# State tiles of a state-space mixer in pairs, the rotation table finished earlier, and modulation pieces in other buffers

## The chip, the cores and the metric

One core of a Trainium2 chip runs the whole program. The metric is the device time of one execution in microseconds, the median over several runs. The profile is of one execution; times in it count from the first instruction of the span.

## The reference

Two blocks run one after the other on `x` (256 tokens by 1024 features, float32). Each has two layers, and each layer a mixer and a feed-forward part, both modulated by six vectors `mod = silu(c) @ mod_w + mod_b`. The change touches the first layer of the first block alone:

```
mod = silu(c) @ mod_w[0] + mod_b[0]            # sh1, sc1, g1, sh2, sc2, g2
h = modulate(rms_norm(x, g), sh1, sc1)
proj = h @ ab_w_in                             # u (512), q, k, v (512 each)
# state-space mixer on u: 32 groups of 16 features, 64 complex states each
bu = einsum(u, b_bar)                          # per state, complex
x_t = a * x_{t-1} + bu_t                       # complex a, over 256 tokens
y = Re(einsum(x, c)) + d * u
y = gelu(y);  y_ssm = y * sigmoid(y @ glu_w + glu_b)
# attention on q, k, v: 8 heads of 64, causal, with a bias table
y = concat(y_ssm, y_att) @ ab_w_out
x = x + g1 * y
```

Everything is computed in float32. Large products are made from a rounded upper part and a rest of each operand (`w_hi`, `w_lo`, `h_hi`, `h_lo`), three matmuls for each product; `ab_in` alone is done with plain float32 matmuls.

## The kernel before

All weights come as a stream of chunks of 128 by 2048 through three `raw` buffers, filled by DMAs that SyncE issues. ScalarE makes `w_hi` (function `hi`, L746) and VectorE `w_lo` (`lo`, L1368) of each chunk, TensorE multiplies. The first eight chunks (`ab_in`) are used straight from `raw`. Chunk 8 is glu, chunks 9 to 12 are ab_out, and then the feed-forward part follows. Each engine's order is written out by hand; semaphores tie them.

**State tiles.** The 2048 complex states lie in 16 tiles of 128 (`j` = 0 to 15). The recurrence with a complex factor is done as a real scan in a frame that turns: `turns_[:, j]` is the table of cosines and sines (`e_re`, `e_im`) of 256 steps for the tile. It is built by doubling: 64 steps for all tiles at the start, then for each tile 64 to 128 (`BASE`) and 128 to 256 (`2 * BASE`), each time two ScalarE copies (`twist`, L884 and L885) and one VectorE instruction (`double`, L1625). For a tile TensorE makes the input (`bu`, L2318, with 32 rows of contraction: row group `j % 4`) into bank `j % 2`; VectorE turns it (`ssm_tile`, L1656 to L1660), scans (L1662) and turns back (L1671, L1673) into `by_cos[j % 2]` and `by_sin[j % 2]`; TensorE takes it through C (`y_of`, L2335, 32 output rows: column group `j % 4`) and adds up in `Y_BANK`, with a skip product (L2329) at every fourth tile. A plain float32 matmul shows as two records. Tiles 0 to 7 have four terms in `y_of`. From tile 8 on GpSimd makes the `by_sin` product (L728) and VectorE combines the parts (`turned_back`, L1682 and L1683), so that two terms remain.

**Order.** In the loop over the 8 chunks of ab_in, TensorE does chunk `c`, `bu(c + 1)` and `y_of(c - 2)`; ScalarE copies chunk `c` out of its bank (L921), converts chunk `c + 3` where that is 8 or more, and twists; VectorE does the conversion's rest, a double, `ssm_tile(c)` and another double. In the loop over 8 heads TensorE does `bu(9 + h)`, `y_of(7 + h)`, the turn of the previous head's probabilities (L2136), the modulation pieces of this head (L2213), the previous head's output (L2397) and the next head's scores (L2377); VectorE does `ssm_tile(8 + h)` with doubles, the reciprocal of the previous head (L1702), this head's bias and maximum (L1693, L1696) and `turned_back`; ScalarE twists, scales the previous head's probabilities (L933), takes the exponential (L961) and copies (L939, L944). Behind the last head ScalarE copies the last part of y (`y_out`, L906), does gelu (L973) and the upper part for the glu product (L976), and TensorE opens the glu banks (L2304).

**Modulation pieces.** `mod` of this layer is 48 pieces of 128 by 1024 (`pm_piece`, L2213), four column groups of 32 at once. Pieces 0 to 15 run before ab_in. Pieces 16 to 47 are loaded into the halves of the three `raw` buffers (6 slots, `pm_late`) after ab_out 0 and 1 have been converted, and used in heads 1 to 7, five for each head (`late_pieces`). Then SyncE goes on with chunk 11.

Of the kernel before, what the change touches and what calls it, by code (L numbers as in the profile page):

```python
# [18 lines left out]
F32 = mybir.dt.float32  # L19
# [53 lines left out]
PM_SLOTS, PM_LATE = 8, 6  # L73
# [184 lines left out]
def build(nc, A, out):  # L258
    with ExitStack() as ctx:
# [12 lines left out]
        w_hi = [sb(f"w_hi{i}", [P, CHUNK], F32R) for i in range(SLOTS)]  # L272
        w_lo = [sb(f"w_lo{i}", [P, CHUNK], F32R) for i in range(SLOTS)]
        x = sb("x", [P, 2, D])
        h_hi, h_lo = sb("h_hi", [P, DT, T], F32R), sb("h_lo", [P, DT, T], F32R)
# [53 lines left out]
        by_cos, by_sin = ([at(PREP + 3072 + 1024 * k + 512 * i, 2, T) for i in range(2)] for k in range(2))  # L329
# [6 lines left out]
        pm_late = [raw[i // 2][:, i % 2 * PM_COLS:(i % 2 + 1) * PM_COLS] for i in range(PM_LATE)]  # L336
# [130 lines left out]
        for m in range(PM_PIECES):  # L467
            k = m % PM_SLOTS if m < PM_FIRST else (m - PM_FIRST) % PM_LATE
# [22 lines left out]
        Y_BANK = (2, 6, 2, 5)  # L491
        DOUBLED = [(j, BASE) for j in range(4)] + [(j, 2 * BASE) for j in range(2)]
        for _c in range(8):
            DOUBLED += [(_c + 4, BASE), (_c + 2, 2 * BASE)]
        for _h in range(6):
            DOUBLED += [(_h + 12, BASE)] * (_h < 4) + [(_h + 10, 2 * BASE)]
# [74 lines left out]
        def _(sp):  # L571
# [48 lines left out]
            def load_pm(m):  # L620
# [3 lines left out]
                n = PM_LATE if first else PM_SLOTS  # L624
                if m >= first + n:
                    sp.wait_ge(sem("pm_used"), m - n + 1)
# [17 lines left out]
            load_plain("ab_in", 2, 6)  # L644
# [6 lines left out]
            sp.wait_ge(hi_done, Q["ab_out"] + 2 - PLAIN)  # L651
            sp.wait_ge(lo_done, Q["ab_out"] + 2 - PLAIN)
            for h in range(1, HEADS):
                for m in late_pieces(h):
                    load_pm(m)
                if h <= 4:
                    load_bias(h + 3)
            sp.wait_ge(sem("pm_used"), PM_PIECES)
# [65 lines left out]
        def _(pool):  # L724
            for j in range(8, ST):
                pool.wait_ge(sem("scan_done"), j - 7)
                pool.wait_ge(*((sem("state_ready"), j - 1) if j >= 10 else (sem("ssm_y_done"), j - 1)))
# [2107 lines left out]
```

## Time and profile before

| | us |
|---|---|
| device time, median of 3 runs | 1533.94 (1531.2 to 1534.71) |
| the profiled execution's time | 1535.15 |
| its span, first to last instruction | 1533.3 |
| TensorE matmuls busy | 1441.6 (94% of the span) |
| VectorE busy | 1089.6 (71%) |
| ScalarE busy | 773.2 (50%) |
| GpSimd busy | 19.6 (1%) |

A busy time is the time in which an engine had an instruction in work; matmuls are pipelined, and their records overlap. A record of the timeline has a start, a length, the engine, the line and the tiles; in brackets stands the idle time of the engine before it and who ended it. The granted clock (PEclk) is TensorE's clock as a share of 2.4 GHz; its low level is 0.5.

### The profile page before, as it was taken

How to read it: one execution, taken by the hardware profiler on the slowest of the kernel's cores; microseconds unless marked ns; L12 is line 12 of the kernel's file. 1: busy time of each engine (PE TensorE's matmuls, PEld its weight loads, DVE VectorE, ACT ScalarE, POOL GpSimd, SP SyncE). 2: the span in 40 equal slices, each digit the busy share in tenths (PEclk: the TensorE clock that was granted, in tenths of full speed). 3: DMA queues.
4: the chain of work that ended last, by engine and by line, in shares of the span. 5: the costliest groups of instructions: out<-in, count | busy, mean ns of one | idle time of the engine just before them, and what ended most of it. 6: DMA issues, size and time to landing. Idle time of an engine off the chain costs nothing.

```text
span 1533.3 us, 24753 instructions
## 1 busy us (share of the span) xinstructions
PE 1441.6 (94%) x9349; PEld 1196.7 (78%) x9363; DVE 1089.6 (71%) x1664; ACT 773.2 (50%) x1142; POOL 19.6 (1%) x14
## 2 busy tenths in 40 slices
PE   6996789999999999999999889999999999999998
PEld 3772458899976668999979755799997877799997
DVE  6657746988894465998985467586667859676666
ACT  4123355545554265555555667565446542455554
POOL 0001100000000000000001000000000000000000
PEclk9996899999999999999999999999999999999999
DMA  9434644888869774898833400355555434345551
GB/s 367 143 108 165 227 183 175 344 326 307 318 245 358 304 290 190 344 370 313 344 147 114 144 6 19 135 192 171 199 178 180 178 110 137 110 165 191 179 198 61
DMA packets 58059, 315.63 MB, mean 206 GB/s; under 512 B 7011, under 2 KB 8524, under 8 KB 33856
## 3 DMA queue, kind: packets, MB, share of 16 engines
q1 hardware_dynamic: 54114, 304.35, 53.7%
q10 hardware_dynamic: 3870, 10.25, 2.2%
q8 instruction: 51, 0.84, 0.2%
q14 instruction: 24, 0.20, 0.0%
HBM read 311.85 MB, written 1.15 MB: 204 GB/s over the span
## 4 chain that ended last, share of the span: by engine, by line
PE 76%; DVE 9%; ACT 5%; issue 5%; DMA 4%; SPq 0%; ACTq 0%; DVEq 0%; POOL 0%
PE bank L2263 60%; PE bank L2356 3%; PE bank L2536 2%; PE bank L2136 2%; ACT w_hi L746 1%; DMA raw<-in_stream 1%; PE bank L2213 1%; DMA arena<-in_mod_pe 1%; DVE w_lo L1368 1%; PE bank L2620 1%; PE bank L2154 1%; DMA arena<-in_mod_later 1%; DVE hf L1524 1%; ACT hf L786 1%; DVE arena L1396 1%
## 5 line engine op out<-in xcount | busy, mean ns | idle before, releaser
L1368 DVE TENSOR_TENSOR w_lo<-raw,w_hi 128x2048 fp32r<-128x2048 f32 x178 | 407.3, 2289 | 180.5 <-ACT w_hi L746 179.6
L2263 PE MATMUL bank<-h_hi,w_hi 128*128 128x256 f32 x1704 | 487.2, 286 | 2.2 <-ACT arena L1229 0.9
L2263 PE MATMUL bank<-h_lo,w_hi 128*128 128x256 f32 x1704 | 482.0, 283 | 0.0
L2263 PE MATMUL bank<-h_hi,w_lo 128*128 128x256 f32 x1704 | 482.0, 283 | 0.0
L746 ACT ACTIVATE w_hi<-raw 128x2048 fp32r<-128x2048 f32 x178 | 340.6, 1914 | 135.7 <-PE bank L2263 110.3
L2263 PEld LDWEIGHTS bank<-h_hi,w_hi 128*128 128x128 f32 x1704 | 326.8, 192 | 9.2 <-issue 4.1
L2263 PEld LDWEIGHTS bank<-h_lo,w_hi 128*128 128x128 f32 x1704 | 326.7, 192 | 2.3 <-issue 0.7
L2263 PEld LDWEIGHTS bank<-h_hi,w_lo 128*128 128x128 f32 x1704 | 326.7, 192 | 0.0
L1786 DVE SCALAR_TENSOR_TENSOR arena<-bank,par,arena 128x255 f32<-128x255 f32 (+1 forms) x264 | 109.1, 475 | 111.0 <-ACT arena L1017 79.3
L2263 PE MATMUL bank<-w_hi,a_hi 128*128 128x512 f32 x368 | 146.0, 397 | 5.0 <-DVE a_lo L1811 4.2
L2263 PE MATMUL bank<-w_hi,a_lo 128*128 128x512 f32 x368 | 144.2, 392 | 0.0
L2263 PE MATMUL bank<-w_lo,a_hi 128*128 128x512 f32 x368 | 143.9, 391 | 0.0
L1017 ACT ACTIVATE arena<-bank,par 128x256 f32<-128x256 f32 x88 | 44.8, 559 | 139.1 <-PE bank L2263 139.1
L1396 DVE SCALAR_TENSOR_TENSOR arena<-arena,silu_c 128x384 f32<-128x384 f32 (+1 forms) x192 | 104.3, 612 | 0.0
L2263 PEld LDWEIGHTS bank<-w_hi,a_hi 128*128 128x128 f32 x368 | 69.5, 189 | 22.2 <-DVE w_lo L1368 5.2
L2263 PE MATMUL bank<-w_hi,h_hi 128*128 128x512 f32 x192 | 76.9, 401 | 5.8 <-DVE hf L1524 3.0
L2263 PEld LDWEIGHTS bank<-w_lo,a_hi 128*128 128x128 f32 x368 | 69.5, 189 | 15.1
L2263 PEld LDWEIGHTS bank<-w_hi,a_lo 128*128 128x128 f32 x368 | 69.7, 189 | 12.9
L2263 PE MATMUL bank<-w_lo,h_hi 128*128 128x512 f32 x192 | 75.3, 392 | 0.0
L2263 PE MATMUL bank<-w_hi,h_lo 128*128 128x512 f32 x192 | 75.3, 392 | 0.0
L2136 PEld LDWEIGHTS bank<-ident_sb,hf 128*128 128x128 f32 x304 | 38.9, 156 | 36.6 <-ACT hf L933 15.8
L2136 PE MATMUL bank<-ident_sb,hf 128*128 128x128 f32 x304 | 47.2, 303 | 19.6 <-ACT hf L933 13.1
(328 smaller groups left out, 1752.7 us busy)
## 6 DMA issues: line engine op xcount, KB each, us to landing
raw<-in_stream SPq DMA_DIRECT2D x186, 1024.0 KB, 5.0
arena<-in_mod_stream SPq DMA_DIRECT2D x64, 768.0 KB, 8.0
arena<-in_mod_later SPq DMA_DIRECT2D x48, 512.0 KB, 7.8
raw<-in_mod_pe SPq DMA_DIRECT2D x40, 512.0 KB, 6.4
arena<-in_mod_pe SPq DMA_DIRECT2D x8, 512.0 KB, 10.0
sq<-row_store ACTq DMA_DIRECT2D x7, 512.0 KB, 3.8
sq<-in_bias SPq DMA_DIRECT2D x8, 256.0 KB, 5.8
x<-in_x_t ACTq DMA_DIRECT2D x1, 1024.0 KB, 8.8
```

The lines of the kernel that those rows point to most:

```text
L746: nc.scalar.activation(w_hi[s][:], raw[s][:], ACT.Copy).then_inc(hi_done, 1)
L786: nc.scalar.activation(hf[:, k, :], turned(n, k), ACT.Identity, **by).then_inc(sem("full_ready"), 1)
L1017: ins = nc.scalar.activation(gate_c[:, e, :], half(4, e), ACT.Identity, scale=par[:, bass.ds(wb[center] + 2 * s + e, 1)], bias=par[:, bass ...
L1368: nc.vector.tensor_tensor(w_lo[s][:], raw[s][:], w_hi[s][:].bitcast(F32), ALU.subtract).then_inc(lo_done, 1)
L1396: ins = nc.vector.scalar_tensor_tensor(parts[e], buf[:, kt % 4, :], silu_c[:, c0 + kt:c0 + kt + 1], parts[e], ALU.mult, ALU.add)
L1524: ins = nc.vector.tensor_tensor(part, acc[:], row_at(gate_rows[gate], fh), ALU.mult)
L1786: ins = nc.vector.scalar_tensor_tensor(o, src, par[:, bass.ds(w[tap] + 2 * s + e, 1)], o, ALU.mult, ALU.add)
L2136: return nc.tensor.transpose(out_, in_, ident[0:n, 0:n])
L2154: nc.tensor.matmul(bank[dst][:], zeros[:, 0:P], zeros[:], start=True, stop=True)
L2263: ins = nc.tensor.matmul(out_, l, r, start=first and n == 0, stop=last and n == 2, **kw)
L2356: ins = nc.tensor.matmul(half(4 + fill % 2, n), *sides, start=c > 0 and k == 0, stop=k == DT - 1, skip_group_check=c == 0)
L2536: ins = nc.tensor.matmul(bank[2 * part + ft][:], dft[:, part, t, ft * P:(ft + 1) * P], sources[part][:, t, 512 * s_:512 * s_ + 512], start ...
```

## The change

- Pieces 16 to 47 go into 8 slots that lie on the memory of `w_hi[0]`, `w_lo[0]`, `w_hi[1]` and `w_lo[1]`. Pieces 16 to 23 are loaded already behind chunk 2 of ab_in, and run in head 0; four follow in each of heads 1 to 6. The conversions of chunks 9 and 10 (ab_out) wait until the pieces are through: ScalarE does them ahead of head 7's probabilities, VectorE behind head 7. Chunk 8 (glu) is converted by ScalarE behind ab_in and by VectorE in head 6.
- The doublings are done in seven steps of four, all within ab_in, by `TWISTS_BEHIND` on ScalarE and `DOUBLE_AHEAD` on VectorE.
- `bu` and `y_of` become `bu_pair` and `y_pair`: two tiles with their instructions in turn, so that neighbours are in different row groups or column groups. The inputs lie in banks 0 and 1, or 3 and 7. Ten tiles are computed in ab_in, the rest in heads 0 to 5.
- GpSimd's product and `turned_back` go; each tile has both products on VectorE and four terms. `by_cos` and `by_sin` have four buffers each; two of them lie on the memory of `h_hi`.

```diff
+        with ExitStack() as early:
+            early_pieces = [early.enter_context(nc.sbuf_tensor(f"early_pieces{i}", [P, CHUNK], F32)) for i in range(4)]
+            early_states = early.enter_context(nc.sbuf_tensor("early_states", [P, DT, T], F32))
+        w_split = [sb(("w_hi", "w_lo")[i % 2] + str(i // 2), [P, CHUNK], F32R) for i in range(4)]
+        h_hi = sb("h_hi", [P, DT, T], F32R)
...
         def late_pieces(h):
-            return range(PM_FIRST + 5 * max(h - 1, 0), min(PM_FIRST + 5 * h, PM_PIECES))
+            first = PM_FIRST + (0, 8, 12, 16, 20, 24, 28, 32)[h]
+            return range(first, min(first + (4 if h else 8), PM_PIECES))
...
+        EARLY = 10
+        BU_BANKS = ((0, 1), (3, 7), (0, 1), (3, 7), (0, 1), (0, 1), (0, 1), (0, 1))
+        BU_BEFORE = (None, None, 0, 1, 2, 4, 5, 6)
+        def doublings(s):
+            return [(j, BASE) for j in range(4 + 2 * s, min(6 + 2 * s, ST))] + [(j, 2 * BASE) for j in (2 + 2 * s, 3 + 2 * s)]
+        TWISTS_BEHIND = {0: (0,), 1: (1,), 3: (2,), 4: (3, 4), 5: (5, 6)}
+        DOUBLE_AHEAD = {1: 0, 3: 1, 5: 2, 6: 3, 7: 4, 8: 5, 9: 6}
...
@@ SyncE @@
-            load_plain("ab_in", 2, 6)
+            load_plain("ab_in", 2, 3)
+            for m in late_pieces(0):
+                load_pm(m)
+            load_plain("ab_in", 3, 6)
...
-            sp.wait_ge(hi_done, Q["ab_out"] + 2 - PLAIN)
-            sp.wait_ge(lo_done, Q["ab_out"] + 2 - PLAIN)
-            for h in range(1, HEADS):
+            for h in range(HEADS - 1):
                 for m in late_pieces(h):
-                    load_pm(m)
...
+                    if m + PM_SLOTS < PM_PIECES:
+                        load_pm(m + PM_SLOTS)
-            sp.wait_ge(sem("pm_used"), PM_PIECES)
...
@@ GpSimd @@
-            for j in range(8, ST):
-                pool.wait_ge(sem("scan_done"), j - 7)
-                nc.gpsimd.tensor_tensor(by_sin[j % 2], rot_b, e_im[:, j, :].unsqueeze(1).broadcast_to([P, 2, T]), ALU.mult)\
...
@@ VectorE @@
+                if j >= 4:
+                    dve.wait_ge(sem("ssm_y_done"), j // 2 - 1)
+                nc.vector.tensor_tensor(by_cos[j % 4], rot_b, er, ALU.mult)
+                nc.vector.tensor_tensor(by_sin[j % 4], rot_b, ei, ALU.mult).then_inc(sem("state_ready"), 1)
...
+            for j in range(EARLY):
+                if j in DOUBLE_AHEAD:
+                    for jj, m in doublings(DOUBLE_AHEAD[j]):
+                        double(jj, m)
+                ssm_tile(j)
             for h in range(HEADS):
+                if h + EARLY < ST:
+                    ssm_tile(h + EARLY)
+                if h == HEADS - 2:
+                    lo_upto(Q["glu"])
                 if h:
                     recip(h - 1)
                 head(h)
+            lo_upto(Q["ab_out"] + 1)
...
@@ TensorE, chunk loop @@
+                if c in (2, 3, 5, 6, 7):
+                    y_pair((2, 3, 5, 6, 7).index(c))
+                if c == 2:
+                    pe.wait_ge(bank_free, FILL["ab_in"] + 2)
+                if c in (2, 3, 4, 6):
+                    bu_pair(2 + (2, 3, 4, 6).index(c))
...
@@ TensorE, head loop @@
+                if h in (1, 3):
+                    bu_pair(6 + h // 2)
                 if h + 1 < HEADS:
                     scores(h + 1)
+                if h in (1, 3, 5):
+                    y_pair(5 + h // 2)
```

## Rows read from the trace of the kernel before

**Rows 1.** Windows: busy us (instructions) of each engine, POOL, granted clock, DMA share, GB/s.
```profile
0.00:38.00 38.00, 24.48 (x170) 11.53 (x172) 26.39 (x113) 15.72 (x40) 0.21 (x4) 1.00 0.94 366
34.00:115.00 81.00, 78.95 (x348) 59.43 (x348) 48.80 (x85) 18.92 (x48) 0.00 (x0) 1.00 0.40 142
115.00:130.00 15.00, 7.33 (x20) 3.12 (x20) 11.62 (x19) 4.70 (x11) 0.52 (x1) 0.66 0.48 180
130.00:144.00 14.00, 9.13 (x34) 4.41 (x38) 11.11 (x20) 5.63 (x16) 3.01 (x2) 0.60 0.17 56
...
176.00:208.00 32.00, 29.36 (x231) 15.35 (x230) 21.27 (x44) 14.92 (x42) 5.96 (x4) 1.00 0.74 265
```

**Rows 2.** Timeline in ab_in: start, length, engine, line, tiles, [idle before <-releaser].
```profile
69.78 1.13 PE L2318 MATMUL bank<-arena 32*128 32x256 f32 x4
...
70.84 1.91 PE L2335 MATMUL bank<-arena 128*32 128x256 f32 x8
...
70.99 0.35 DVE L1625 SCALAR_TENSOR_TENSOR arena<-arena 128x128 f32<-128x128 f32 x1 [5.13 <-ACT arena L885]
...
71.26 0.68 DVE L1656 TENSOR_TENSOR arena<-bank,arena 128x512 f32<-128x512 f32 x1
...
72.68 7.17 PE L2356 MATMUL bank<-raw,hf 128*128 128x256 f32 x32
...
76.01 0.48 DVE L1625 SCALAR_TENSOR_TENSOR arena<-arena 128x256 f32<-128x256 f32 x1
```

**Rows 3.** Timeline, TensorE: small matmuls that stand side by side.
```profile
42.06 1.14 PE L2318 MATMUL bank<-arena 32*128 32x256 f32 x8 [0.78 <-ACT arena L921]
...
123.94 5.33 PE L2335 MATMUL bank<-arena 128*32 128x256 f32 x16
...
188.63 1.93 PE L2213 MATMUL bank<-raw,arena 128*32 128x256 f32 x32
```

**Rows 4.** Timeline around the conversions in ab_in and the first head.
```profile
94.58 1.91 ACT L746 ACTIVATE w_hi<-raw 128x2048 fp32r<-128x2048 f32 x1 [4.09 <-DMA raw<-in_stream]
...
96.52 2.29 DVE L1368 TENSOR_TENSOR w_lo<-raw,w_hi 128x2048 fp32r<-128x2048 f32 x1 [10.03 <-ACT w_hi L746]
...
113.86 1.13 PE L2377 MATMUL bank<-arena 64*128 64x256 f32 x4
...
121.94 2.07 PE L2318 MATMUL bank<-arena 32*128 32x256 f32 x4 [6.95 <-DVE arena L1657]
```

**Rows 5.** Timeline in heads 1 and 2.
```profile
132.19 1.47 PE L2377 MATMUL bank<-arena 64*128 64x256 f32 x4 [2.91 <-DVE hf L1693]
...
147.69 1.13 PE L2377 MATMUL bank<-arena 64*128 64x256 f32 x4
...
148.69 0.35 DVE L1625 SCALAR_TENSOR_TENSOR arena<-arena 128x128 f32<-128x128 f32 x1 [6.36 <-ACT arena L885]
```

**Rows 6.** Timeline in heads 5 to 7.
```profile
184.32 1.13 PE L2377 MATMUL bank<-arena 64*128 64x256 f32 x4
...
186.10 0.67 DVE L1693 SCALAR_TENSOR_TENSOR hf<-bank,sq 128x512 f32<-128x512 f32 x1
...
186.22 0.91 ACT L933 ACTIVATE hf<-hf,small 128x256 f32<-128x256 f32 x2 [0.29 <-DVE small L1702]
...
188.04 0.66 PE L2136 MATMUL bank<-ident_sb,hf 128*128 128x128 f32 x4
...
192.17 1.08 PE L2397 MATMUL bank<-hf,arena 128*64 128x256 f32 x4
...
200.51 1.13 PE L2377 MATMUL bank<-arena 64*128 64x256 f32 x4
```

**Rows 7.** Timeline: GpSimd's product and the double beside it.
```profile
152.42 1.77 POOL L728 TENSOR_TENSOR arena<-arena 128x512 f32<-128x512 f32 x1 [12.43 <-DVE arena L1662]
...
153.10 1.36 DVE L1625 SCALAR_TENSOR_TENSOR arena<-arena 128x256 f32<-128x256 f32 x1
```

**Rows 8.** Timeline: the first upper part of glu's input.
```profile
210.16 0.63 ACT L976 ACTIVATE a_hi<-arena 128x512 fp32r<-128x512 f32 x1
```

More of the change, by code:

```diff
@@ L328, in build @@
         silu_wide = at(PREP + 2560, DT, 32)
-        by_cos, by_sin = ([at(PREP + 3072 + 1024 * k + 512 * i, 2, T) for i in range(2)] for k in range(2))
+        by_cos, by_sin = ([at(PREP + 3072 + 1024 * k + 512 * i, 2, T) for i in range(2)] +
+                          [early_states[:, 4 * k + 2 * i:4 * k + 2 * i + 2, :] for i in range(2)] for k in range(2))
         b_turned = at(PREP + 5120, 2, UT, P)
@@ L467, in build @@
         for m in range(PM_PIECES):
-            k = m % PM_SLOTS if m < PM_FIRST else (m - PM_FIRST) % PM_LATE
+            k = m % PM_SLOTS
             _n_[k] += 16
@@ L623, in load_pm @@
                 first = 0 if m < PM_FIRST else PM_FIRST
-                n = PM_LATE if first else PM_SLOTS
-                if m >= first + n:
-                    sp.wait_ge(sem("pm_used"), m - n + 1)
+                if m >= first + PM_SLOTS:
+                    sp.wait_ge(sem("pm_used"), m - PM_SLOTS + 1)
                 sp.dma_start(buf, A["mod_pe"][m]).then_inc(landed, 16)
@@ L921, in _ @@
                 nc.scalar.activation(dst, src, ACT.Copy).then_inc(bank_free, 1)
-                hi_upto(q + 3)
-                twist(c + 4, BASE)
-                twist(c + 2, 2 * BASE)
-                if c == 6:
+                if c == 4:
                     y_out(0)
+                for s in TWISTS_BEHIND.get(c, ()):
+                    for j, m in doublings(s):
+                        twist(j, m)
+            hi_upto(Q["glu"])
+            y_out(1)
             pT = [hf[:, 4 + 2 * i:6 + 2 * i, :] for i in range(2)]
@@ L2329, in y_of @@
                     nc.tensor.matmul(half(Y_BANK[n], 0), skip_diag[:, n, :], u_t[:, n, :], start=True, stop=False, skip_group_check=True)
-                c_, s_ = by_cos[j % 2], by_sin[j % 2]
-                terms = [(0, c_[:, 0, :]), (1, c_[:, 1, :])]
-                if j < 8:
-                    terms += [(2, s_[:, 1, :]), (1, s_[:, 0, :])]
-                for i, (e, v) in enumerate(terms):
-                    ins = nc.tensor.matmul(half(Y_BANK[n], 0)[r:r + 32, :], c_turned[:, e, n, r:r + 32], v, start=False, stop=(i == len(terms) - 1),
-                                           skip_group_check=True)
+                for i, (e, part) in enumerate(((0, 0), (1, 1), (2, 1), (1, 0))):
+                    for j in (2 * p, 2 * p + 1):
+                        r = 32 * (j % 4)
+                        v = (by_cos if i < 2 else by_sin)[j % 4][:, part, :]
+                        ins = nc.tensor.matmul(half(Y_BANK[n], 0)[r:r + 32, :], c_turned[:, e, n, r:r + 32], v, start=False, stop=i == 3,
+                                               skip_group_check=True)
                 ins.then_inc(sem("ssm_y_done"), 1)
@@ L2374, in scores @@
                     pe.wait_ge(sem("scores_used"), h)
+                else:
+                    pe.wait_ge(sem("bu_used"), 8)
                 r = slice(64 * (h % 2), 64 * (h % 2) + 64)
```

110 lines of the change are left out of this document (33 added, 77 removed).

## The prediction

> **What bounds the kernel now.** I read the page's share of TensorE first, then the windows by stage, then the timeline of the two stretches that the change touches. Everything edited runs before the glu projection, in the first 212 us of 1533; what follows starts from semaphores of that stretch, so it should only shift. Two stages matter. In ab_in (34 to 114 us) TensorE is busy 78.95 of 81 us at full clock and bounds [rows 1]. VectorE is busy 48.8 us of them, mostly waiting. In the head stage (114 to 210 us) nobody is busy throughout: TensorE has 7.33 of 15 us at its start at a granted clock of 0.66 (0.60 in the window behind it), and 29.36 of 32 us at 1.00 near its end [rows 1]. So that stage is a ring of waits through ScalarE, VectorE and TensorE, and what counts is which operations lie on the ring.
>
> **Ab_in before.** One period is 10.0 us on TensorE: 7.1 us of chunk, 1.05 us of `bu` (69.78 to 70.84), 1.85 us of `y_of` (70.84 to 72.68) [rows 2]. One state tile on VectorE, from its first rotation to the double behind it, is 71.26 to 76.01 = 4.75 us [rows 2], both by_cos and by_sin included. So VectorE has room for more than the one tile per chunk it gets.
>
> **Pairs.** The change gives `bu` for two tiles in two row groups and the four y terms for two tiles in two column groups. Are they concurrent? Rows: `bu(0)` and `bu(1)` stand back to back in two row groups: 8 records in 1.14 us, where 4 records of one tile take 1.13 us [rows 2, 3]. So two row groups cost what one does. For columns, 32 records of four pieces in four column groups take 1.93 us, and `y_of(6)` with `y_of(7)`, 16 records, take 5.33 us at the low clock, where a serial 16 would be near 6.8 us (twice the 1.7 us of eight records, twice over for the clock) [rows 2, 3]. I take 1.05 us for a bu pair (up to 1.9 if serial) and 1.85 us for a y pair (up to 3.55).
>
> The Trainium skill, TensorEngine Tiling (Array Packing), Key Properties, says that changing the tiling mode drains TensorE, which speaks against scattering small operations between chunks. The change makes fewer such switches, and whatever one costs is inside the 1.05 and 1.85 us already. By the same page's Gotcha 1, row tiles may not share a bank at once; the pair uses two banks, as the agreeing row of 1.14 us did.
>
> **Ab_in after, step by step.** TensorE: chunk 0 ends 41.2; pairs 0 and 1 use all four row groups (1.05, the copy's wait 0.75 as before); chunk 1 to 50.1, no wait for its copy; chunk 2 to 57.2; then the skip product (two records, 0.43 us at y's pace, and a hand-over of 0.2), y pair 0, bu pair 2 (3.5) to 60.8; chunk 3 to 67.9; y 1 and bu 3 (2.9) to 70.8; chunk 4 to 77.9; bu 4 (1.05); chunk 5 to 86.1; skip and y 2 (2.5); chunk 6 to 95.6; y 3 to 97.5. VectorE starts tile 0 at 43.1. With 4.75 us a tile and about 1.3 us for a step of four doubles (two of 0.27 us, 70.99 to 71.26 [rows 2], and two of 0.39, the record's 0.48 less the same overlap), tiles 1, 3 and 5 end at 53.9, 64.7 and 75.9. It then waits 3.6 us for the twists behind chunk 4's copy; tile 7 ends 92.3, tile 8 98.3, and tile 9 frees its banks at 100.4. **This is the new stall**: bu pair 5 shares banks 0 and 1 with pair 4, so TensorE stands from 97.5 to 100.4 (3 us) with chunk 7 queued behind. Chunk 7 then ends 108.6, skip and y 4 take 2.5, and `scores(0)` starts at 111.1 instead of 113.86 [rows 4]. Gain 2.8 us, with two tiles more done than before (10 computed, where 7 were). The weights' conversions leave ab_in: before, VectorE stood idle 10.03 us until the glu chunk's upper part (itself behind a DMA) and delayed the tile [rows 4]; that wait goes.
>
> **What else moves.** Pieces 16 to 23 (4 MB) go into SyncE's queue behind chunk 2 at about 32 us. At 366 GB/s [rows 1] that is 11.5 us; chunk 3 lands near 55 us and is needed at 60.8. Cover 6 us. The rest of the pieces are fetched eight ahead, on triggers `pm_used`; at 1.4 us each they land before the 6 to 11 us until their head. Loads of ab_out 2 wait for the glu chunk's lower part in head 6 (about 157 us), used 30 us later: nothing. The two conversions of ab_out (1.9 us on ScalarE, 2.29 on VectorE each [rows 4]) come in head 7, on the ring there: 3.8 us of ScalarE count in full, VectorE's 4.6 us lie beside.
>
> **The head stage before.** `scores(1)` and `scores(2)` stand at 132.19 and 147.69: 15.5 us a head. ScalarE copies the head, twists, VectorE's double ends a wait of 6.36 us, and only then may the tile run [rows 5]. From `scores(0)` to `scores(1)` it is 18 us, since TensorE sat 6.95 us until VectorE's tile 7 behind the conversions [rows 4]. From 184.32 to 200.51, two heads later and with no doubles left, it is 8.1 us a head [rows 6]. GpSimd's 1.77 us product lies beside, but a double next to it takes 1.36 us instead of 0.48 [rows 2, 7]: 0.9 us in four heads.
>
> The Trainium skill (GPSIMD Engine Reference, Key points) says that GpSimd shares SBUF interfaces with VectorE, which such a double shows. It changes no term here.
>
> **The head stage after.** All doubles are done, so the ring is: recip, probs 0.97 (ScalarE), turn 0.6, pieces 1.8 (with a piece turn 0.6 in some heads), head_out 1.0, then, in heads 1 and 3, bu pair 1.05, after which VectorE's tile 4.75 leads to the next recip [rows 2, 6]. TensorE's part to the tile's start is 6.3 us, the period 11.0 us; in the other heads VectorE alone counts: the bias add 0.67 and the maximum over the same elements, 1.35 together [rows 6], plus the tile, 6.1 us. **New wait:** VectorE idles 4.9 us in heads 2 and 4 for a bu pair placed behind head_out; queued behind that wait are recip and the bias. Laid out: tile 11 runs in head 1 and gives recip 0 at 118.4; tile 12 begins 124.7; recips 1, 2, 3, 4 at 129.4, 135.5, 146.5, 152.6; scores(6) 159.0; scores(7) begins 164.1. From scores(7) to the upper part of glu's input was 200.51 to 210.16 = 9.7 us [rows 6, 8]; plus 3.8 of conversions, less about 3 for the last tile's GpSimd product and y, 10.5: so 174.6. Before 210.16. **Sum at full clock: 35.6 us** (2.8 in ab_in, 32.8 in the heads).
>
> **The clock.** Before, the granted clock averaged 0.66 and 0.60 in 115 to 144 us [rows 1], a mix of the full 2.4 GHz and of 1.2 GHz, with TensorE idle 6.95 us at one place [rows 4] and 2.91 us at another [rows 5] ahead of the low stretches; from 176 us, busy 29.36 of 32, it is 1.00 [rows 1]. In my layout TensorE's gaps are 2.8, 3.1, 1.7, 2.5, 1.8 and, at the conversions, 4 us. Those near 3 us are like the 2.91 us row, with more work ahead of them than that one had. A ring pass at the low clock costs up to 3.9 us more (turn, pieces, head_out and bu pair doubled); the same layout with every TensorE operation 1.5 times as long ends 9.8 us later, twice as long 25 us later. I take 5 us. So 35.6 - 5 = 30.6, say 31 us.
>
> The page TensorE: Matmul & The Clock Gate (Part 1) of the Trainium skill has idleness bring the low level and sustained work the high one; these rows agree, and by it alone the low clock would return at some gaps.
>
> **From span to time.** The profiled execution took 1535.15 us (span 1533.3); the median is 1533.94. 1534 - 31 = **1503 us**.
>
> **Rivals.**
> 1. *Clock stays high*: gain 34 to 37, 1497 to 1500. For: work per time rises. Chance 0.25; it lies with the forecast (gain 28 to 34, chance 0.42) on one scale.
> 2. *Clock stays low for the whole stage*: gain 35.6 - 25 = 11, to 26 for 1.5: 1508 to 1523. For: five gaps over 1.7 us. Against: 176 to 208 us at 1.00. Chance 0.18.
> 3. *The pairs do not run side by side* (the change does not do what it says): bu serial costs 7 us by the same layout, both serial 15: 1510 to 1518. Against: rows 3. Chance 0.07.
> 4. *Nothing gained*: some wait later in the layer is fixed in time, for instance the ffn0 chunks' DMA. Against: SyncE starts those behind `h_ready`. 1534, chance 0.03.
> 5. *Slower*: serial pairs together with the low clock throughout. Both serial at twice the length ends 49 us after the full-clock layout, 35.6 - 49 = -14: 1548. It decides once the mean ring pass takes over 12 us (96.3 us for eight heads before [rows 4, 8]). Chance 0.03. The last 0.02 go to unseen gains below 1497.
>
> **Range.** 1496 to 1518 holds the first two cases, most of the low clock's and of the serial one's. A difference of 0.2% (3 us) is about what a measurement can tell from no change: faster 0.94, same 0.03, slower 0.03.
>
> **What would show it.** Chunk 7 ending near 109 behind a 3 us gap for VectorE's tile 9 (ab_in right); L2318's and L2335's successors with 8 and 16 records in about 1.1 and 1.9 us (pairs right); head periods of 11 and 6 us alternating, VectorE idle about 5 us before tiles 12 and 14 (ring right); two ScalarE conversions before the last softmax; the granted clock between 115 and 175. Wrong if the chunks wait for DMA, if the glu stage does not begin at 175 to 182, or if what follows is not a plain shift.

## The result, and the profile after

| | before | after |
|---|---|---|
| device time, median | 1534.33 us (1531.2 to 1537.16, 4 runs) | 1508.53 us (1507.53 to 1508.65, 4 runs) |
| the profiled execution's time, span | 1535.15, 1533.3 us | 1508.61, 1505.9 us |
| TensorE matmuls busy | 1441.6 us | 1416.6 us |
| GpSimd busy | 19.6 us | 5.5 us |
| mean granted clock | 0.977 | 0.982 |

After to before is 0.9831 (95% interval 0.9811 to 0.9851): the change makes the kernel 25.8 us faster. The forecast was 1503 us in 1496 to 1518. Sign and range hold; the point was 5.5 us too low.

For the place of the gain I use one marker, the start of the first upper part of glu's input [rows 8]. It stood at 210.16 us and now stands at 180.09: 30.1 us are gained there, where 35.6 at full clock less 5 for the clock were forecast. The same instruction pairs further on stand 30.4 us apart at 460 us (time of before), 29.7 at 820, 26.6 at 861 and 27.3 at 1528. So some 3 us are lost again in one later stage (820 to 861) that the change doesn't touch.

First the changed kernel's stretches by the windows of its trace (start and end, length, busy us and instructions of TensorE, weight load, VectorE, ScalarE and GpSimd, granted clock, DMA share, GB/s), the lines that answer to [rows 1]:

```profile
34.00:115.00 81.00, 76.83 (x394) 59.74 (x394) 66.68 (x127) 24.32 (x73) 0.00 (x0) 0.96 0.51 190
112.00:128.00 16.00, 13.31 (x134) 7.20 (x132) 7.36 (x13) 7.91 (x16) 0.00 (x0) 0.89 0.88 325
128.00:144.00 16.00, 11.29 (x113) 6.53 (x112) 12.10 (x22) 6.49 (x18) 0.00 (x0) 1.00 0.82 310
...
160.00:176.00 16.00, 11.11 (x102) 5.88 (x95) 8.56 (x10) 10.24 (x21) 0.00 (x0) 0.95 0.32 103
176.00:190.00 14.00, 10.42 (x62) 8.92 (x61) 2.27 (x4) 7.94 (x16) 0.00 (x0) 0.69 0.35 135
```

VectorE's work in 34 to 115 us went from 48.80 to 66.68 us: the doubles and two more tiles lie there, under chunks that bind anyway. In the heads the granted clock is 0.89 to 1.00, where it was 0.60 and 0.66 [rows 1], though TensorE is busy for only 11.1 to 13.3 of 16 us. The low level now lies elsewhere: inside 34 to 115 (0.96, where it was 1.00), and at the glu product (0.69, where the same stretch of before, 206 to 220 us, has 0.88).

The timeline of ab_in in the changed kernel (start, length, engine, line, tiles, idle time before and its releaser). L2312 is the `bu` pair, L2328 the `y` pair, L2349 a chunk:

```profile
34.33 8.86 PE L2349 MATMUL bank<-hf,raw 128*128 128x256 f32 x32 [1.06 <-ACT hf L908]
...
43.97 1.16 PE L2312 MATMUL bank<-arena 32*128 32x256 f32 x16 [0.78 <-ACT arena L933]
...
59.50 1.92 PE L2328 MATMUL bank<-arena 128*32 128x256 f32 x16
...
81.09 0.75 DVE L1635 SCALAR_TENSOR_TENSOR arena<-arena 128x128 f32<-128x128 f32 x2 [3.46 <-ACT arena L897]
...
102.08 1.49 PE L2312 MATMUL bank<-arena 32*128 32x256 f32 x8 [3.06 <-DVE arena L1667]
...
103.50 8.46 PE L2349 MATMUL bank<-raw,hf 128*128 128x256 f32 x32
```

Read it from the right: the bracket of 102.08 is the new stall, 3.06 us until VectorE's tile 9 has read its banks (L1667), and the chunk queued behind it takes 8.46 us. A chunk at full clock takes 7.17 [rows 2]; chunk 0, in the first row, took 8.86 here. The bracket of 81.09 is VectorE's wait for twists. The pairs cost 1.9 us for 16 records of y, and 1.16 us for the first sixteen of `bu`.

Heads 0 to 4 in the same trace; L1698 is a head's reciprocal, L1666 a tile's first operation, L2374 the next scores:

```profile
121.47 0.17 DVE L1698 RECIPROCAL small<-small 128x2 f32<-128x2 f32 x1
...
123.84 3.27 PE L2205 MATMUL bank<-early_pieces,arena 128*32 128x256 f32 x32
...
128.06 1.13 PE L2312 MATMUL bank<-arena 32*128 32x256 f32 x8
...
129.30 0.69 DVE L1666 TENSOR_TENSOR arena<-bank,arena 128x512 f32<-128x512 f32 x1 [6.33 <-PE bank L2312]
...
134.05 0.17 DVE L1698 RECIPROCAL small<-small 128x2 f32<-128x2 f32 x1
...
140.23 0.17 DVE L1698 RECIPROCAL small<-small 128x2 f32<-128x2 f32 x1
...
146.44 0.69 DVE L1666 TENSOR_TENSOR arena<-bank,arena 128x512 f32<-128x512 f32 x1 [4.69 <-PE bank L2312]
...
151.19 0.17 DVE L1698 RECIPROCAL small<-small 128x2 f32<-128x2 f32 x1
```

From reciprocal to reciprocal it is 12.6, 6.2, 11.0 us, where the heads of before that still had doubles took 15.5 us [rows 5]. VectorE stands 6.33 and 4.69 us ahead of tiles 12 and 14, each time for a `bu` pair. The tail, where ab_out's conversions have moved to:

```profile
169.21 3.71 ACT L758 ACTIVATE w_hi<-raw 128x2048 fp32r<-128x2048 f32 x2
...
173.78 0.66 PE L2128 MATMUL bank<-ident_sb,hf 128*128 128x128 f32 x4 [3.94 <-ACT hf L947]
...
175.38 1.97 PE L2394 MATMUL bank<-hf,arena 128*64 128x256 f32 x4 [0.95 <-ACT hf L953]
...
180.09 0.63 ACT L986 ACTIVATE a_hi<-arena 128x512 fp32r<-128x512 f32 x1
```

TensorE idles 3.94 us for the probabilities, which ScalarE makes behind the conversions, and the head output behind that takes 1.97 us instead of 1.08 [rows 6].

### The profile page after: what moved, and what is told of

It is laid out like the page before. It is cut to its first block, busy times and chain, and to the rows that moved or that the text cites. A ratio compares the mean times of both kernels' runs of the same rounds, so it can differ in the third digit from the quotient of the medians.

```text
span 1505.9 us, 24787 instructions
## 1 busy us (share of the span) xinstructions
PE 1416.6 (94%) x9381; PEld 1187.9 (79%) x9395; DVE 1084.9 (72%) x1656; ACT 772.8 (51%) x1142; POOL 5.5 (0%) x6
## 4 chain that ended last, share of the span: by engine, by line
PE 73%; DVE 11%; ACT 6%; issue 6%; DMA 4%; SPq 0%; ACTq 0%; DVEq 0%
PE bank L2255 58%; PE bank L2349 3%; PE bank L2531 2%; DVE w_lo L1378 2%; ACT w_hi L758 2%; DMA raw<-in_stream 1%; PE bank L2128 1%; DMA arena<-in_mod_pe 1%; PE bank L2615 1%; DVE arena L1406 1%; PE bank L2205 1%; DVE hf L1534 1%; DMA arena<-in_mod_later 1%; ACT hf L798 1%; ACT hf L1295 1%
## 5 line engine op out<-in xcount | busy, mean ns | idle before, releaser
L758 ACT ACTIVATE w_hi<-raw 128x2048 fp32r<-128x2048 f32 x178 | 340.6, 1914 | 122.2 <-PE bank L2255 111.1
L2255 PEld LDWEIGHTS bank<-w_hi,a_lo 128*128 128x128 f32 x368 | 69.2, 188 | 12.8
```

Of the source, the lines that this page charges most:

```text
L758: nc.scalar.activation(w_hi[s][:], raw[s][:], ACT.Copy).then_inc(hi_done, 1)
L2255: ins = nc.tensor.matmul(out_, l, r, start=first and n == 0, stop=last and n == 2, **kw)
```

## The experiments

Each kernel was run beside the kernel before on its own chip, whose median there lay between 1534 and 1537 us. "Marker" is the start of the first upper part of glu's input in the profiled execution; the next column is the stretch from the start of `scores(0)` to it, the head stage. What lies behind the marker is nearly the same work in all kernels, yet it is no constant: from there to the last instruction the thirteen other profiles took from 3.4 us less to 5.9 us more than that of before. The marker leaves that out, but it is one reading of one execution. Two profiles of the changed kernel lie 0.7 us apart at the marker, and 1.9 and 2.6 us apart, in opposite directions, in the two stretches ahead of it. So a difference of up to about 3 us between two rows is not by itself the doing of an edit.

| kernel | time, us | ratio to before (95%) | marker, us | from `scores(0)`, us | marker against |
|---|---|---|---|---|---|
| before | 1534.33 | | 210.16 | 96.3 | |
| table alone | 1517.95 | 0.9893 (0.9847 to 0.9939) | 189.57 | 76.1 | before: -20.6 |
| no GpSimd product alone | 1538.67 | 1.0005 (0.9979 to 1.003) | 211.38 | 97.1 | before: +1.2 |
| pieces alone | 1535.18 | 0.9990 (0.9962 to 1.0017) | 205.15 | 92.3 | before: -5.0 |
| table, no GpSimd | 1525.21 | 0.9931 (0.9909 to 0.9952) | 197.59 | 82.9 | table alone: +8.0 |
| table and pieces | 1504.49 | 0.9799 (0.9763 to 0.9836) | 177.65 | 65.0 | table alone: -11.9 |
| the change | 1508.53 | 0.9831 (0.9811 to 0.9851) | 180.09 | 65.9 | table and pieces: +2.4 |
| the change, once more | 1507.68 | 0.9827 (0.9801 to 0.9853) | 180.81 | 68.6 | the change: +0.7 |
| pairs tile by tile | 1512.62 | 0.9861 (0.9812 to 0.9909) | 187.75 | 71.9 | the change: +7.7 |
| input pairs ahead | 1496.23 | 0.9752 (0.9705 to 0.9798) | 168.37 | 56.4 | the change: -11.7 |
| pair 5's own banks | 1504.41 | 0.9807 (0.9759 to 0.9855) | 176.85 | 69.7 | the change: -3.2 |
| conversions late | 1505.32 | 0.9812 (0.9765 to 0.9859) | 177.30 | 62.8 | the change: -2.8 |
| gaps filled | 1506.21 | 0.9816 (0.9795 to 0.9837) | 178.69 | 66.1 | the change: -1.4 |
| the three edits on waits together | 1490.31 | 0.9708 (0.9686 to 0.9730) | 161.54 | 54.4 | the change: -18.6 |

### Which part brings the time

**The table alone.** All doublings in ab_in, everything else as before:

```diff
-        for _c in range(8):
-            DOUBLED += [(_c + 4, BASE), (_c + 2, 2 * BASE)]
+        for _s in range(7):
+            DOUBLED += doublings(_s)
...
             for h in range(HEADS):
-                if h < 4:
-                    double(12 + h, BASE)
                 ssm_tile(8 + h)
-                if h < 6:
-                    double(10 + h, 2 * BASE)
```

> The kernel before with one part alone: the doublings of the rotation table in seven steps of four within ab_in, nothing of them in the heads. Theory A (the doubles lie on the ring of the heads, where VectorE waited 18 us in all for ScalarE's twists in five places): 12 to 20 us faster than before, about 1519, and the head period behind the first head falls from 15 to about 10 us. Rival B (the wait only moves, to the tile's input or to the scores): less than 5 us faster, over 1529. In ab_in nothing changes, since VectorE idles there.

The marker came 20.6 us earlier, 20.2 of them behind `scores(0)`, and the time fell to 0.9893 (16.4 us; the profiled execution was the fastest of four). The ring through twist and double was the head stage's bound, as read from [rows 5].

**GpSimd's product alone.** Both products on VectorE and four y terms for every tile, without pairs:

```diff
-            for j in range(8, ST):
-                pool.wait_ge(sem("scan_done"), j - 7)
...
-                terms = [(0, c_[:, 0, :]), (1, c_[:, 1, :])]
-                if j < 8:
-                    terms += [(2, s_[:, 1, :]), (1, s_[:, 0, :])]
+                terms = [(0, c_[:, 0, :]), (1, c_[:, 1, :]), (2, s_[:, 1, :]), (1, s_[:, 0, :])]
```

> The kernel before with one part alone: no product on GpSimd, both products of every tile on VectorE and four terms for every tile on TensorE, tiles still one by one with two buffers. Theory A (GpSimd lay beside; its removal pays 0.9 us in four heads and 0.1 us a tile, and costs 0.85 to 1.7 us of TensorE a head, partly idle): between 3 us faster and 3 us slower, 1534. Rival C (GpSimd carried a good part of the gain): 8 us or more faster, 1526.

Theory A: no difference, 1.0005. While the doubles set the pace, neither GpSimd's 1.77 us nor the two extra y terms are on the path.

**The pieces alone.** The slots of the weight split, the pieces ahead of the heads, the conversions in heads 6 and 7:

```diff
-        pm_late = [raw[i // 2][:, i % 2 * PM_COLS:(i % 2 + 1) * PM_COLS] for i in range(PM_LATE)]
+        pm_late = [early_pieces[i // 2][:, i % 2 * PM_COLS:(i % 2 + 1) * PM_COLS] for i in range(PM_SLOTS)]
...
-                hi_upto(q + 3)
...
+                if h == HEADS - 1:
+                    hi_upto(Q["ab_out"] + 1)
```

> The kernel before with one part alone: modulation pieces 16 to 47 in eight slots on the memory of the weight parts, eight of them in head 0 and four in each of heads 1 to 6, glu's conversion behind ab_in and in head 6, ab_out's in head 7. Theory A (the conversions in ab_in delay tiles 5 to 7 and with them the first head by about 12 us, and cost 3.8 us in head 7): 6 to 12 us faster, about 1525. Rival D (the first head then waits for the doubles instead, and the conversions in head 7 take the rest back): within 3 us of before.

Theory A missed: 5.0 us at the marker, and nothing in the time that can be told from no change (0.9990), which is rival D's. In the profiled execution the 5.0 us are lost again behind the marker. The first head starts 9 us sooner than before (`scores(1)` at 123.00 against 132.19 [rows 5]), but VectorE then waits for the twists just as it did. Its waits in the timeline of this kernel:

```profile
140.34 0.35 DVE L1632 SCALAR_TENSOR_TENSOR arena<-arena 128x128 f32<-128x128 f32 x1 [6.94 <-ACT arena L890]
...
154.36 0.35 DVE L1632 SCALAR_TENSOR_TENSOR arena<-arena 128x128 f32<-128x128 f32 x1 [6.19 <-ACT arena L890]
```

**The table without GpSimd's product.** The first two edits together, no pairs:

> The kernel before with two parts together: the table finished in ab_in, and no product on GpSimd. Theory A (the two are nearly additive; without the doubles the GpSimd detour comes nearer to the ring): as the table alone, or up to 4 us faster than that, 1515 to 1519. Rival C: 8 us or more faster than the table alone.

The edit is the diffs of the table and of GpSimd's product. It fits no theory: 8.0 us later at the marker than the table alone, although the same removal had cost nothing that can be told before. (The medians are 7.3 us apart, but their intervals overlap.) With the doubles gone, TensorE's queue is on the ring. The timeline of the table kernel, then that of this one; L1693 and L1681 are the bias add that waits for the next head's scores:

```profile
156.65 0.69 DVE L1693 SCALAR_TENSOR_TENSOR hf<-bank,sq 128x512 f32<-128x512 f32 x1 [0.68 <-PE bank L2374]
...
157.60 1.05 PE L2332 MATMUL bank<-arena 128*32 128x256 f32 x4
```

```profile
162.18 0.69 DVE L1681 SCALAR_TENSOR_TENSOR hf<-bank,sq 128x512 f32<-128x512 f32 x1 [1.61 <-PE bank L2356]
...
163.13 1.91 PE L2314 MATMUL bank<-arena 128*32 128x256 f32 x8
```

Four y terms of one tile take 1.91 us where two take 1.05, ahead of the turn, the pieces and the next scores. 0.86 us for each of the eight tiles from tile 8 on is 6.9 us, and from `scores(0)` to the marker this kernel takes 6.8 us longer. The other 1.2 of the 8.0 us lie ahead of `scores(0)`, where the two kernels are the same. A cost of zero in one state of the kernel was no cost of zero in the next.

**The table and the pieces.** The change without its pairs, GpSimd's product kept (the diffs of the table and of the pieces together):

> The kernel before with the table's doublings all in ab_in and with the later pieces in the weight-split slots (so the weights' conversions leave ab_in too), but with single tiles and with GpSimd's product as before: the changed kernel without its pairs. The table alone brought glu's upper input part from 210.2 to 189.6 us, the pieces alone to 205.2, the whole change to 180.1: 9.5 us are left between the table alone and the change. Theory A, these 9.5 us are the conversions' (once the doubles are gone, a later tile has nothing to hide behind): the part is there at 180 to 183 us, the time is 1508 to 1512 us, and the pairs are worth 3 us or less. Theory B, they are the pairs' (eight of the sixteen tiles leave the heads' ring to two in four heads): the pieces bring again 5 us or less, the part is there at 184.5 to 190 us, the time is 1512 to 1518 us.

Theory A's direction, and beyond its end: the marker at 177.65 and 1504.49 us. The pieces are worth 11.9 us where the table is finished, and 5.0 where it isn't (11.1 and 4.0 behind `scores(0)`). And the pairs, as the change has them, bring nothing that shows: this kernel is 2.4 and 3.2 us ahead of the two profiles of the whole change at the marker, and neither that nor the times, whose intervals overlap, tell it from equal. Heads 2 and 3 in its timeline, and the marker:

```profile
130.67 0.17 DVE L1709 RECIPROCAL small<-small 128x2 f32<-128x2 f32 x1
...
136.92 0.17 DVE L1709 RECIPROCAL small<-small 128x2 f32<-128x2 f32 x1
...
143.26 0.17 DVE L1709 RECIPROCAL small<-small 128x2 f32<-128x2 f32 x1
...
177.65 0.63 ACT L983 ACTIVATE a_hi<-arena 128x512 fp32r<-128x512 f32 x1
```

6.25 and 6.34 us a head, with VectorE hardly idle (0.8 us in all from 113 to 166 us): a tile's input is always ready, since each `bu` stands a head ahead of its tile. The pairs take two tiles out of the heads, and put waits of 6.33 and 4.69 us in front of two others.

### Whether the pairs run side by side

The changed kernel with the same instructions, ordered tile by tile:

```diff
-                for e in range(2):
-                    for i in range(2):
...
+                for i in range(2):
...
+                    for e in range(2):
...
-                for i, (e, part) in enumerate(((0, 0), (1, 1), (2, 1), (1, 0))):
-                    for j in (2 * p, 2 * p + 1):
+                for j in (2 * p, 2 * p + 1):
+                    for i, (e, part) in enumerate(((0, 0), (1, 1), (2, 1), (1, 0))):
```

> The changed kernel with the instructions of each pair ordered tile by tile: first all of one tile, then all of the other. Theory A (row and column groups work through their own instructions side by side, as bu(0) and bu(1) did in 1.14 us when issued tile by tile): the pairs keep about 1.1 and 1.9 us and the time stays at 1508.5, within 2 us. Rival E (only neighbours in the program overlap): a y pair takes about 3.5 us and a bu pair 1.9, worked as 15 us more in all, 1520 to 1524.

The timeline of this kernel:

```profile
104.53 1.14 PE L2312 MATMUL bank<-arena 32*128 32x256 f32 x8 [1.29 <-DVE arena L1667]
...
113.14 2.81 PE L2328 MATMUL bank<-arena 128*32 128x256 f32 x16
```

It fell between the theories. The input pair takes 1.14 us in either order, so two row groups run together even when their instructions aren't neighbours one by one. The y pair takes 2.81 us instead of 1.92, so the two column groups run fully side by side only when their instructions alternate; why part of the overlap is left in the other order was not measured. The marker moved by 7.7 us. Eight y pairs at 0.9 us each would be 7.1, but that is not how it came about. The five pairs in ab_in moved `scores(0)` by only 1.7 us, since the longer pairs fill the stall ahead of input pair 5 (1.29 us instead of 3.06), and the chunk behind it takes 7.17 us again. The other 6.0 us lie in the heads, where three pairs account for 2.7; there the granted clock is low in other places too, and what that costs was not separated.

### The three waits

**Input pairs 6 and 7 ahead of the head's other TensorE work:**

```diff
             for h in range(HEADS):
+                if h in (1, 3):
+                    bu_pair(6 + h // 2)
                 if h:
                     head_turn(h - 1)
...
-                if h in (1, 3):
-                    bu_pair(6 + h // 2)
```

> The changed kernel with bu pairs 6 and 7 ahead of the turn of the probabilities instead of behind head_out, in heads 1 and 3. Theory A (VectorE's idle 6.3 and 4.7 us before tiles 12 and 14 are on the ring, because TensorE issues the pair last): both vanish, all head periods with a tile are 6 to 7 us, and the marker before glu comes 8 to 10 us earlier; 1499. Rival F (the wait is handed on to the scores or to the turn): 3 us or less.

Theory A: the marker 11.7 us earlier, 1496.23 us. Of these, 9.5 us lie behind `scores(0)`, in A's 8 to 10; the other 2.2 came with chunk 0, which began 0.6 us earlier in this profile and ran at full clock, and which the edit doesn't touch. The reciprocals in its timeline:

```profile
125.42 0.17 DVE L1698 RECIPROCAL small<-small 128x2 f32<-128x2 f32 x1
...
133.10 0.17 DVE L1698 RECIPROCAL small<-small 128x2 f32<-128x2 f32 x1
...
139.46 0.17 DVE L1698 RECIPROCAL small<-small 128x2 f32<-128x2 f32 x1
...
145.65 0.17 DVE L1698 RECIPROCAL small<-small 128x2 f32<-128x2 f32 x1
```

None of 11 or 12 us is left: the head from 125.42 has 7.7, with 1.4 us of waiting for late scores behind a low clock, the others 6.2 to 6.4. Two lines further up in TensorE's order were worth more than the pairs had been: only now are the heads shorter than with table and pieces alone (56.4 against 65.0 us).

**Pair 5 in banks 3 and 7:**

```diff
-        BU_BANKS = ((0, 1), (3, 7), (0, 1), (3, 7), (0, 1), (0, 1), (0, 1), (0, 1))
-        BU_BEFORE = (None, None, 0, 1, 2, 4, 5, 6)
+        BU_BANKS = ((0, 1), (3, 7), (0, 1), (3, 7), (0, 1), (3, 7), (0, 1), (0, 1))
+        BU_BEFORE = (None, None, 0, 1, 2, 3, 4, 6)
...
-                    pe.wait_ge(sem("bu_used"), 8)
+                    pe.wait_ge(sem("bu_used"), 11)
```

> The changed kernel with bu pair 5 in banks 3 and 7, so that it need not wait for tile 9. Theory A (the 3.06 us gap before chunk 7 is a wait for banks, and brings the low clock that makes chunk 7 8.46 us long): no gap, chunk 7 in 7.2 us, scores(0) 4 us earlier at about 110; VectorE then has tile 10 later than the scores, so 1 to 4 us remain at the end. Rival G (VectorE is the bound of that stretch): scores(0) earlier, but the time within 1 us of 1508.5.

Its timeline where the stall was:

```profile
96.69 1.13 PE L2312 MATMUL bank<-arena 32*128 32x256 f32 x8
97.75 7.17 PE L2349 MATMUL bank<-raw,hf 128*128 128x256 f32 x32
...
107.14 1.13 PE L2374 MATMUL bank<-arena 64*128 64x256 f32 x4
```

The gap is gone, the chunk takes 7.17 us again, and `scores(0)` comes 7.0 us earlier than in the changed kernel (2.3 of them because chunk 0 began 0.6 us earlier and ran at full clock this time). But only 3.2 us arrive at the marker; between the two the granted clock is 0.85 (windows, 110 to 170 us) where the changed kernel's profile has 0.96 (112 to 176 us), while the order of the work is the same. The second profile of the changed kernel has 0.87 in 112 to 176 us, so the edit need not be the reason. Theory A for the gap; its 1 to 4 us are there in the medians, but the intervals overlap with the changed kernel's.

**ab_out's conversions behind glu's input:**

```diff
-                if h == HEADS - 1:
-                    hi_upto(Q["ab_out"] + 1)
...
             act.dma_start(at(ARENA - 512, 64 + P), A["mod_pick"]).then_inc(sem("row_stored"), 16)
+            hi_upto(Q["ab_out"] + 1)
...
             attention_lower(0)
+            lo_upto(Q["ab_out"] + 1)
```

> The changed kernel with ab_out's two conversions behind the input of the glu product instead of ahead of head 7's probabilities. Theory A (3.7 us of ScalarE lie on the ring there, with a 3.9 us gap of TensorE and the low clock behind it): the marker before glu 3.7 to 5 us earlier, of which up to 2 us come back at ab_out, 1504 to 1506. Rival H (they only hide in other waits): within 1 us of 1508.5.

Theory A's direction, somewhat short of it: the marker came 2.8 us earlier (3.2 from `scores(0)` on), and 2.5 us of it are still there at 228 us (time of before). In the times the intervals overlap. In the prediction the conversions were to cost 3.8 us, all of ScalarE's part.

### What the gaps do to the clock

Twelve products of zeros ahead of input pair 5, sixteen ahead of head 6's turn, both into a free bank:

```diff
+                if c == 6:
+                    pe.wait_ge(sem("y_ready"), 1)
+                    stay_awake(12, 2)
                 if c in (2, 3, 4, 6):
...
+                if h == HEADS - 1:
+                    pe.wait_ge(sem("y_ready"), 3)
+                    stay_awake(16, 2)
                 if h:
                     head_turn(h - 1)
```

> The changed kernel with idle TensorE time filled at two places: twelve products of zeros (512 columns, into a free bank) ahead of input pair 5, where the profile has a gap of 3.06 us and then chunk 7 at the low clock (8.46 us instead of 7.2), and sixteen of them in head 7 ahead of head 6's turn, where the gap is 3.94 us and the clock is low from 174.4 to 184.6 us. Nothing else moves. Theory A, the low clock follows from these gaps: chunk 7 takes 7.2 us again, scores(0) comes 1.3 us earlier than 114.2, glu's input part 1 to 3 us earlier than 180.1, and the time is 1504 to 1508 us. Theory B, the clock falls at those places whatever TensorE does there: chunk 7 stays at 8.4 us, the fill itself costs up to 1 us, and the time is within 1.5 us of the changed kernel's 1508.5.

The timeline of this kernel at both places:

```profile
99.03 2.76 PE L2146 MATMUL bank<-zeros 128*128 128x512 bf16 x12
102.18 1.13 PE L2312 MATMUL bank<-arena 32*128 32x256 f32 x8 [0.38 <-DVE arena L1667]
103.25 7.17 PE L2349 MATMUL bank<-raw,hf 128*128 128x256 f32 x32
...
169.24 3.63 PE L2146 MATMUL bank<-zeros 128*128 128x512 bf16 x16
...
174.87 1.08 PE L2397 MATMUL bank<-hf,arena 128*64 128x256 f32 x4 [0.95 <-ACT hf L953]
...
180.22 1.01 PE L2296 MATMUL bank<-zeros 128*128 128x512 bf16 x2 [3.09 <-DVE a_lo L1719]
```

Theory A for the cause. Nothing but the gap's content changed at 99 us, pair 5 starts at the same time to 0.1 us (102.18 against 102.08), and the chunk behind takes 7.17 us instead of 8.46. In the tail the head output is back at 1.08 us. The low level at the glu product then starts in the next gap, 3.09 us ahead of it. The Trainium skill (TensorE: Matmul & The Clock Gate, Part 1) has idleness bring the low level; here the trace agrees, with 1.3 us saved on the chunk by filling one gap. Head 1 gave some of it back in this profile: the low level lasted longer there, and the head took 13.6 us instead of 12.6. In time it is 2 us (1506.21 against 1508.53), which these intervals don't tell apart.

The changed kernel once more:

> The changed kernel once more, unchanged. Theory A, where the clock falls is set by the program: chunk 0 again takes 8.9 us instead of 7.2, chunk 7 8.4 us, glu's input part is there at 180 us, and the stage of the attention's low-rank projections again gives back 3 us against the kernel before. Theory B, the clock falls where it happens to: chunk 0 has 7.2 us this time, the marker differs by over 1 us, and the give-back in the later stage is another size or gone. The time is 1505 to 1511 us by both.

1507.68 us, ratio 0.9827 (0.9801 to 0.9853), marker 180.81. Both theories hold in a part of it. Chunk 0 took 7.17 us this time, so its 8.86 in the first profile is not a property of the change. Chunk 7, behind the same stall, took 8.86 us (8.46 in the first profile), so that one is. But not every such gap has the low level behind it. Head 2's turn and pieces, in the first profile and in the second:

```profile
135.21 0.66 PE L2128 MATMUL bank<-ident_sb,hf 128*128 128x128 f32 x4 [3.12 <-ACT hf L947]
135.80 1.93 PE L2205 MATMUL bank<-early_pieces,arena 128*32 128x256 f32 x32
```

```profile
133.32 1.11 PE L2128 MATMUL bank<-ident_sb,hf 128*128 128x128 f32 x4 [3.13 <-ACT hf L947]
134.36 3.64 PE L2205 MATMUL bank<-early_pieces,arena 128*32 128x256 f32 x32
```

The same gap in the same program had no slow work behind it in one execution, and some 2 us of it in the other. What decides between the two was not found. The later stage gave back 3 us again. That stage in windows of the same work, in the trace of before, of after, of after once more, and of the table with the pieces:

```profile
786.00:861.50 75.50, 70.32 (x538) 65.57 (x540) 44.64 (x69) 43.46 (x77) 5.26 (x2) 1.00 0.37 117
```

```profile
756.00:834.00 78.00, 73.04 (x534) 67.75 (x534) 44.37 (x67) 43.48 (x77) 5.25 (x2) 0.96 0.36 118
```

```profile
755.50:834.00 78.50, 72.91 (x535) 67.57 (x532) 44.84 (x69) 43.46 (x77) 5.25 (x2) 0.96 0.37 116
```

```profile
754.00:829.70 75.70, 70.66 (x542) 65.79 (x542) 44.82 (x68) 43.47 (x77) 5.27 (x2) 1.00 0.38 117
```

TensorE has the same work and is busy for 2.7 us longer at a granted clock of 0.96 instead of 1.00. The kernel with the input pairs ahead has 1.00 there, the one with all three edits 0.96. So the 3 us are the clock's, and they come or stay away with programs that differ only hundreds of microseconds earlier. What decides it there wasn't found. The Trainium skill (same page and part) has the clock gate's watch on activity run free, without a reset when a kernel starts; chunk 0's 8.86 and 7.17 us in two profiles of one program agree with that.

### All three edits together

> The changed kernel with the three edits of the last runs together: the last two input pairs of the state tiles ahead of their heads' other TensorE work, pair 5 in its own two banks, and the conversions of ab_out's weights behind glu's input. Each alone brought glu's upper input part forward against the changed kernel's 180.1 us: by 11.7, by 3.2 and by 2.0 us. Theory A, the three waits are one behind the other on the same ring (a gap in front of head 0, a gap in heads 2 and 4, a delay in head 7): the gains add, the part is there at 162 to 165 us, the time is 1488 to 1494 us. Theory B, with the input pairs ahead the ring is bound by VectorE's tiles, and an earlier scores(0) or a shorter head 7 is given back at a softmax or a tile: the part at 167 us or later, the time no less than 1495 us.

The edit is the three diffs on the waits. Theory A: the marker at 161.54 (from 180.09 less 11.7, 3.2 and 2.8 it would be 162.4; the first two both contain the 2.2 us of chunk 0, so counted once it would be 164.6; the expectation's 2.0 for the conversions is 2.8 by the marker's row), 1490.31 us, 0.9708 (0.9686 to 0.9730). That is the fastest kernel here, 18.2 us under the changed one.

## Why the prediction was right, and where its sizes were off

**What bounds the kernel.** Right. Taking the twists and doubles out of the heads brought 20.6 us at the marker by itself, taking away anything else first brought 5 us or nothing.

**The pairs' durations.** Right: 1.13 us for a `bu` pair, 1.92 for a y pair (1.05 and 1.85 were taken as their part of the period). Rival 3 (pairs serial) is out for the row groups. For the column groups it would have been half true with another order: 2.81 us.

**Ab_in.** The stall for tile 9 was forecast at 3 us and measured 3.06, VectorE's wait for the twists at 3.6 and measured 3.46. `scores(0)` was forecast at 111.1 and came at 114.17. The layout has no error of that size. 1.7 us are chunk 0 at the low clock (8.86 against 7.17), which the second profile doesn't have; 1.3 are chunk 7 behind the stall and 0.4 pair 5 itself (1.49 against 1.13). The term that was mis-sized is the price of the stall: it was put down as 3 us idle, and it cost 3.06 idle and 1.65 of slow work behind it, which the text had reckoned only for the heads. The second profile, with chunk 0 at full clock, confirms the layout: the stall lies from 97.03 to 100.11 us (forecast 97.5 to 100.4), and `scores(0)` comes at 112.25.

**Cover for what moved.** The waits of TensorE in 34 to 200 us name no DMA, so pieces 16 to 23 in SyncE's queue stayed inside their cover, as forecast.

**The heads.** From `scores(0)` to the marker 63.5 us were forecast, 65.9 measured. Periods of 11.0 and 6.1 us were forecast, and 11.0 and 6.2 measured wherever the clock was high. Head 1's was 12.6, with its pieces at 3.27 us instead of 1.93 [rows 3]. VectorE's waits ahead of tiles 12 and 14, forecast at 4.9, were 6.33 (that head) and 4.69. The tail has 0.9 us more for the head output and 0.5 for the piece turn, again the clock. The conversions were priced at 3.8 us and cost 2.8, or 3.2 from `scores(0)` on.

**The clock.** Forecast at 5 us up to the marker, for the heads. The slow work that the rows show is 1.7 (chunk 0), 1.65 (pair 5 and chunk 7), 1.5 (head 1) and 1.4 (tail), 6.2 us in all. With them back, the marker would have gained 36.3 us, where the layout at full clock has 35.6. So the sum of the parts was right to 1 us, and the term for the clock too small by about 1 us up to there. The second profile has its slow work elsewhere (head 3 took 12.8 us, chunk 0 none) and gains 29.4 us; by the difference from the same 36.3 the clock cost 6.9 us there. The forecast's mechanism is the one that the rows show: clock low at some gaps, neither high nor low throughout. Its band is not: 28 to 34 us holds the marker's 30.1, but the time gained 25.8, which lies just outside it, and at the upper end of the 11 to 26 us that rival 2 had for another reason. That the single number came within 5.5 us is sound reckoning up to the marker, and a missing term behind it.

**From the marker to the time.** This is the term with the largest error. The text took everything behind the marker for a plain shift, and named the contrary as a sign of being wrong. 2.7 us were lost there between the marker and the last instructions, mostly in one stage that the change leaves alone, by the clock. Another 0.9 us is the time around the span (1535.15 less 1533.3 before, 1508.61 less 1505.9 after). With 0.9 us at the marker these are the 4.5 us between 31 and the 26.5 of the two profiled executions; the rest of the 5.5 is the median beside the profiled time.

**What the sum hid.** The prediction laid out the whole change and never a part without the others, so it could not see that its gain isn't shared evenly: table and pieces give 32.5 us at the marker, and the pairs with GpSimd's product gone give -2.4 on top, which is nothing within what two profiles of one kernel differ by. The text had the two 11 us periods with 4.9 us of idle VectorE in them. It took them as the change's price, when one `bu` pair further ahead removes them.

## What to carry to other kernels

Price each part of a change with and without the others, since the same part was worth 5.0 or 11.9 us, and another 0 or 8.0, by what else was on the ring. When pairing or grouping work makes fewer, larger steps, look where the first step of the group stands in the producer's queue: an input issued behind work that depends on the previous head took back all that the pairs had gained. And allow for a gap of about 3 us on TensorE costing more than its length: the one ahead of chunk 7 cost 4.7, in head 2 the same length cost nothing more in one execution and some 2 us more in the next. Last, read a marker of one profile against a second profile of the same kernel before a difference of 2 or 3 us is given to an edit.

## What the runs showed of the hardware

- Sixteen float32 matmul records with 32 output rows, in two column groups, take 1.92 us when the groups alternate and 2.81 us when they don't; eight records of one tile take 1.91. Row groups don't need the order: 1.13 us for one tile's four records, 1.13 or 1.14 for two tiles' eight in either order, and 1.16 for sixteen in all four row groups.
- The gap of 3.06 us on TensorE ahead of chunk 7 is followed by the low clock in both profiles of the changed kernel (a chunk of 8.46 and 8.86 us). With 2.76 us of zero products in it the chunk takes 7.17. A gap of 3.12 us in head 2 is followed by the low clock in one of the two profiles, and not in the other.
- In a stage of unchanged work the granted clock is 0.96 in three of the profiles shown or named here and 1.00 in three (before among them), which is 2.5 to 3 us. Both profiles of the changed kernel have 0.96, and the one with only the input pairs moved has 1.00, so it may follow from what runs earlier; what decides it stays open.
